# Prompt attention: division of the probabilities moved from VectorE to GpSimd, half of the transposed copies moved to VectorE, copies issued ahead of the exponentials

## The chip, the cores and the metric

The kernel is one launch on one core of one Trainium2 chip. The core has five engines that each run their own instruction list in order and meet only at semaphores: TensorE (PE) for matrix products, VectorE (DVE), ScalarE (ACT), GpSimd (POOL) and SyncE (SP), which only starts transfers. The metric is device microseconds from start to end of the one launch. Before the change three runs took 1468.16, 1467.0 and 1467.94 us, the median is 1467.94 us.

## What is computed

One decoder layer for a prompt of 512 rows and for 8 sequences that decode 4 rows each (32 rows, with a cache of 2048 rows). The layer is a SwiGLU half, a projection into all heads, two kinds of attention, an output projection, a second SwiGLU half and a gated embedding. The part that the change touches is the attention of the prompt: 12 heads of mixer A, which see every key at or before the query with a table of biases, and 4 heads of mixer B, which see the 128 best keys by a separate score. Cut to one head and one block of queries:

```
logits = q @ k.T + bias            # bias holds -1e30 where a key must not be seen
m      = logits.max(-1)
pr     = exp(logits - m)
l      = pr.sum(-1)
o      = (pr / l) @ v
```

The three dilated patterns of mixer A are folded into one softmax by adding the log of how often a key occurs to its bias. Mixer B divides by its own denominator in the same way.

## The kernel before, in words

The dense stages before and after attention work on all 544 rows and are not touched. Prompt attention runs between them and the decode attention. It has 32 steps. Step m takes head pair q = m // 4 (heads 2q and 2q+1) and block of queries i = m % 4, 128 queries each; since a query sees no later key, block i has 128 * (i + 1) keys. So four steps make a group (one head pair) with 128, 256, 384 and 512 key columns. Groups 0 to 5 are mixer A, groups 6 and 7 mixer B. A step goes through these pieces, each for both heads (h2 = 0 and 1):

- `scores(m)` on PE (line 1965) puts q @ k.T into a PSUM bank.
- VectorE adds the bias and takes the row minimum of the negated sum (line 1381), into one of six tiles `LP`, so a tile is free again three steps later.
- ScalarE takes the exponential in place and sums the row (line 931).
- `normalise(m)` on VectorE takes the two reciprocals (line 1358) and scales both tiles (line 1361).
- `transposed(m)` on PE (line 1975) turns the probabilities, 128 x 128 at a time, into two PSUM banks, one for each head.
- ScalarE copies both banks to `PTS` (line 940).
- `values(m)` on PE (line 1987) multiplies with the value rows. After four steps VectorE takes the group's output out (`take_out`, line 1365).

Nothing plans the order; each engine's order is written out. In round m PE does scores(m), transposed(m-2), values(m-3). ScalarE does the exponentials of step m and then the copies of step m-2. VectorE does the logits of step m, then normalise(m-1), and after every fourth step take_out. After the logits of step 10 VectorE also builds the query blocks for decoding (`decode_queries`, lines 1333 to 1350).

GpSimd has two tasks here. After the logits of each of the groups 0 to 5 it issues four transfers that load the bias tables of the head pair after next (`load_bias`, line 666). For the mixer B groups it adds the top-k mask to the bias (`mask_bias`, line 696), for blocks 1 to 3 of each group, and the logits of those blocks wait for that sum in `TM`. `TM` holds one block for each of the two heads, so the next block's sum waits until the logits have read the last one.

Decode attention follows on VectorE's list right behind the last take_out: VectorE starts the top-k rounds of the decode rows (lines 1402, 1403, 1457) there.

## Time and profile before

| | us |
|---|---|
| median of three runs | 1467.94 (1467.0 to 1468.16) |
| profiled execution, its own time | 1468.33 |
| span of the profiled execution | 1466.7 |
| PE busy in the span | 1375.8 (94%) |
| VectorE busy | 551.8 (38%) |
| ScalarE busy | 449.5 (31%) |
| GpSimd busy | 627.5 (43%) |

The span is what the hardware profiler recorded from the first to the last instruction, and 1.6 us of the execution's own time lie outside it. The shares of busy time are means over stages that are limited by different things. Prompt attention covers 641.0 us (the first scores) to 730.5 us (the end of the last take_out), 89.5 us or 6% of the span, and only that stretch tells what the change can do.

### The profile page before, as it was taken

The numbers are of one execution on the slowest core, as the hardware profiler recorded it, in microseconds if no ns is written. First come the engines' busy times: TensorE is split into PE (matmuls) and PEld (weight loads), VectorE is DVE, ScalarE is ACT, GpSimd is POOL, SyncE is SP. The second block draws the span as 40 slices with busy tenths as digits, with TensorE's granted clock in tenths as the row PEclk, the third lists the DMA queues.
The fourth block names the chain that finished last, engine by engine and source line by source line (L and its number), as shares of the span: only waits on it lengthen the run. The fifth ranks groups of instructions, "written<-read, shape, count | busy, mean of one in ns | idle before, by whom it ended". The sixth has DMA issues, their size and how long they took to land.

```text
span 1466.7 us, 30734 instructions
## 1 busy us (share of the span) xinstructions
PE 1375.8 (94%) x12059; PEld 1269.4 (87%) x12059; DVE 551.8 (38%) x1340; ACT 449.5 (31%) x833; POOL 627.5 (43%) x431
## 2 busy tenths in 40 slices
PE   6999999999989999997877897989999999999988
PEld 6999999999979988965555565979999999999888
DVE  5222222200242246777899524162222222110454
ACT  2122222211262333246644431153222222111441
POOL 6343333455465645321455003544333333554642
PEclk9999999999989999999999998989999999999999
DMA  6298755766355533331199898434565657665221
GB/s 231 86 269 316 257 197 208 250 230 213 124 180 170 157 87 102 137 103 53 41 277 283 259 319 312 137 133 167 192 208 192 215 192 269 213 222 173 70 70 47
DMA packets 95775, 269.83 MB, mean 184 GB/s; under 512 B 36306, under 2 KB 36691, under 8 KB 95161
## 3 DMA queue, kind: packets, MB, share of 16 engines
q1 hardware_dynamic: 89000, 255.34, 52.0%
q0 software_dynamic: 5632, 10.50, 2.6%
q10 hardware_dynamic: 1040, 2.62, 1.2%
q8 instruction: 66, 1.08, 0.3%
q14 instruction: 37, 0.30, 0.1%
HBM read 259.78 MB, written 109.10 MB: 252 GB/s over the span
## 4 chain that ended last, share of the span: by engine, by line
PE 81%; DVE 8%; POOL 4%; ACT 2%; issue 2%; DMA 2%; SPq 1%; ACTq 0%; DVEq 0%; POOLq 0%
PE bank L1615 22%; PE bank L1619 21%; PE bank L1617 21%; POOL w_rest L576 2%; DVE idx_scores L1457 2%; DMA cache_a_ring<-in_cache_a 2%; PE bank L1663 1%; PE bank L2158 1%; PE bank L1975 1%; PE bank L1965 1%; PE bank L1665 1%; PE bank L1664 1%; PE bank L1987 1%; DVE idx_scores_left L1403 1%; POOL x_rest L586 1%
## 5 line engine op out<-in xcount | busy, mean ns | idle before, releaser
L576 POOL TENSOR_TENSOR w_rest<-w_raw,w_high 128x1024 fp32r<-128x1024 f32 (+2 forms) x159 | 410.3, 2581 | 596.4 <-ACT w_high L751 595.5
L751 ACT ACTIVATE w_high<-w_raw 128x1024 fp32r<-128x1024 f32 (+2 forms) x159 | 180.2, 1134 | 778.0 <-PE bank L1619 746.0
L1615 PE MATMUL bank<-x_high,w_high 128*128 128x272 f32 x1808 | 378.1, 290 | 13.1 <-POOL x_rest L586 11.7
L1619 PE MATMUL bank<-x_high,w_rest 128*128 128x272 f32 x1808 | 374.6, 289 | 0.0
L1617 PE MATMUL bank<-x_rest,w_high 128*128 128x272 f32 x1808 | 373.4, 288 | 0.0
L1615 PEld LDWEIGHTS bank<-x_high,w_high 128*128 128x128 f32 x1808 | 284.3, 189 | 21.4 <-issue 16.6
L1617 PEld LDWEIGHTS bank<-x_rest,w_high 128*128 128x128 f32 x1808 | 284.8, 189 | 0.0
L1619 PEld LDWEIGHTS bank<-x_high,w_rest 128*128 128x128 f32 x1808 | 282.8, 189 | 0.0
L1058 DVE SCALAR_TENSOR_TENSOR hidden<-silu_gate,bank 128x272 f32<-128x272 f32 x88 | 34.5, 434 | 389.3 <-ACT silu_gate L771 389.3
L1615 PE MATMUL bank<-hidden_high,w_high 128*128 128x272 f32 x616 | 127.7, 288 | 0.0
L1619 PE MATMUL bank<-hidden_high,w_rest 128*128 128x272 f32 x616 | 127.5, 288 | 0.0
L1617 PE MATMUL bank<-hidden_rest,w_high 128*128 128x272 f32 x616 | 127.0, 288 | 0.0
L1615 PEld LDWEIGHTS bank<-hidden_high,w_high 128*128 128x128 f32 x616 | 97.0, 188 | 0.2
L1617 PEld LDWEIGHTS bank<-hidden_rest,w_high 128*128 128x128 f32 x616 | 96.8, 188 | 0.0
L1619 PEld LDWEIGHTS bank<-hidden_high,w_rest 128*128 128x128 f32 x616 | 96.2, 189 | 0.0
L1079 DVE SCALAR_TENSOR_TENSOR y<-y,bank 128x272 f32<-128x272 f32 x42 | 16.5, 434 | 208.1 <-PE bank L1619 179.4
L2032 PE MATMUL bank<-consts_sb,cache_a_ring 128*128 128x128 f32 x336 | 52.5, 297 | 23.9 <-DMA cache_a_ring<-in_cache_a 22.9
L2032 PEld LDWEIGHTS bank<-consts_sb,cache_a_ring 128*128 128x128 f32 x336 | 38.8, 149 | 37.3 <-DMA cache_a_ring<-in_cache_a 31.7
L398 POOL DMA_DIRECT2D kv_b_pages<-in_cache_b x64 | 46.3, 723 | 40.3 <-issue 40.3
L1062 DVE CAST hidden_high<-hidden 128x544 f32 (+1 forms) x44 | 49.1, 1116 | 7.8 <-DVE hidden L1058 3.5
L955 ACT ACTIVATE k_a_t<-bank 128x512 f32<-128x512 f32 x56 | 33.4, 597 | 54.7 <-PE bank L2032 54.7
L718 POOL TENSOR_TENSOR attn_out_rest<-attn_out_t,attn_out_high 128x512 fp32r<-128x512 f32 x8 | 10.5, 1331 | 89.6 <-DVE attn_out_high L1506 89.6
(317 smaller groups left out, 1875.2 us busy)
## 6 DMA issues: line engine op xcount, KB each, us to landing
out_a_sample<-in_cache_a SPq DMA_DIRECT2D x73, 1344.0 KB
w_raw<-in_w_wi SPq DMA_DIRECT2D x88, 512.0 KB, 5.2
cache_a_ring<-in_cache_a SPq DMA_DIRECT2D x112, 384.0 KB, 4.8
w_raw<-in_w_wo SPq DMA_DIRECT2D x32, 704.0 KB, 5.3
w_raw<-in_w_w_in SPq DMA_DIRECT2D x26, 512.0 KB, 3.7
w_raw<-in_w_gate SPq DMA_DIRECT2D x8, 640.0 KB, 3.9
bias_toeplitz<-rev_bias POOLq DMA_DIRECT2D x32, 128.0 KB, 2.6
kv_b_pages<-in_cache_b POOLq DMA_DIRECT2D x64, 64.0 KB, 4.1
```

The source lines that it names most:

```text
L398: eng.dma_start(KVP[:, :, q, :], cache_b[bass.ds(page, 1), :, 0:2 * HD].rearrange("o p (s n) -> (o p) s n", s=2)).then_inc(kv_in[g // 4 + ...
L576: nc.gpsimd.tensor_tensor(rest_part(u0, i, j)[:, 0:tiles, :], RAW[:, slot, 0:tiles, :], high_part(u0, i, j)[:, 0:tiles, :].bitcast(F32), A ...
L751: nc.scalar.activation(high_part(u0, i, j)[:, 0:tiles, :], RAW[:, slot, 0:tiles, :], ACT.Copy).then_inc(S["hi_ready"], 1)
L955: nc.scalar.activation(KTA[:, n % 2, 0:512], BANK[b0][:, :], ACT.Copy)
L1058: last = v.scalar_tensor_tensor(half(HF, s, n), half(SG, s, n), 0.5, BANK[4 * s + 2 + n][:, 0:HALF], ALU.mult, ALU.mult)
L1062: v.tensor_copy(HH[:, bass.ds(c, 1), :], HF[:, s:s + 1, :]).then_inc(S["hh_done"], 1)
L1079: last = v.scalar_tensor_tensor(half(Y, m, n), half(Y, m, n), ALPHA, BANK[2 * (m % 2) + n][:, 0:HALF], ALU.mult, ALU.add)
L1457: own.done(v.match_replace(SC[:], TOP[:, 8 * r:8 * r + 8], SC[:], PASSED))
L1615: mm(banks[n][:, 0:HALF], wh, xh[n], start=start, stop=False)
L1617: mm(banks[n][:, 0:HALF], wh, xl[n], start=False, stop=False)
L1619: last = mm(banks[n][:, 0:HALF], wl, xh[n], start=False, stop=stop)
L2032: last = tr(BANK[2 * (n % 2) + c // 4][:, 128 * (c % 4):128 * (c % 4) + 128], AR[:, n % KEY_RING, 128 * c:128 * c + 128], IDENT)
```

## The change

The reciprocals stay on VectorE, but for the first 24 steps (groups 0 to 5) the scaling by them is done by GpSimd, one instruction for each head, which waits for VectorE's reciprocals through a new semaphore `inv_done`. For the same steps the transposed probabilities of the second head are copied from PSUM by VectorE (`keep_pt`) instead of ScalarE. On ScalarE the copies of step m-2 now stand ahead of the exponentials of step m, in all 32 steps. GpSimd's bias loads stand behind the division of each group's fourth step, and its first two mask sums (group 6, block 1) stand between the divisions of steps 22 and 23. PE's waits follow: `probs_ready` and `pt_kept` name the semaphore of the engine that did the work.

```
+            def divide(m):
+                c, nk = 44 + 2 * m % 6, 128 * (m % 4 + 1)
+                pool.wait_ge(S["inv_done"], m + 1)
+                for h2 in range(2):
+                    l = LP[(2 * m + h2) % 6][:, 0:nk]
+                    nc.gpsimd.tensor_scalar(l, l, SMALL[:, c + h2:c + h2 + 1], None, ALU.mult
+                                            ).then_inc(S["probs_done_p"], 1)
...
-            for q in range(6):
-                pool.wait_ge(S["logits_done"], 8 * (q + 1))
+            for m in range(POOL_STEPS):
+                divide(m)
+                if m % 4 == 3:
+                    for h2 in range(2):
+                        load_bias(m // 4 * 2 + 4 + h2)
+                if m == POOL_STEPS - 2:
+                    for h2 in range(2):
+                        mask_bias(HEADS_A // 2, 1, h2)
...
+            def invert(m):
+                dve.wait_ge(S["exp_done"], 2 * m + 2)
+                c = 38 + 2 * m % 6
+                v.reciprocal(SMALL[:, c + 6:c + 8], SMALL[:, c:c + 2]).then_inc(S["inv_done"], 1)
+
+            def keep_pt(k):
+                nk = 128 * (k % 4 + 1)
+                dve.wait_ge(S["pt_ps"], 2 * k + 2)
+                if k >= 2:
+                    dve.wait_ge(S["pv_done"], 2 * k - 2)
+                v.tensor_copy(PTS[:, k % 2, 1, 0:nk], BANK[3][:, 0:nk]).then_inc(S["pt_sb_d"], 1)
...
-                if m >= 1:
+                if 0 < m <= POOL_STEPS:
+                    invert(m - 1)
+                elif m > POOL_STEPS:
                     normalise(m - 1)
+                if 0 <= m - 2 < POOL_STEPS:
+                    keep_pt(m - 2)
...
-                    pe.wait_ge(S["probs_done"], n + 1)
+                    pe.wait_ge(*probs_ready(n))
                     if m >= 1:
-                        pe.wait_ge(S["pt_sb"], n - 1)
+                        pe.wait_ge(*pt_kept(m - 1, h2))
```

On ScalarE, around the last step of group 4 and the first of group 5, each round of before puts two exponentials ahead of two copies (`logits_96` to `logits_101` are the six `LP` tiles, `probs_t` is `PTS`):

```order
L931 ACTIVATE logits_98,small<-logits_98,small 128x384 [waits logits_done]
L931 ACTIVATE logits_99,small<-logits_99,small 128x384 [waits logits_done]
L940 ACTIVATE probs_t<-bank 128x128 [waits pv_done,pt_ps] x2
L931 ACTIVATE logits_100,small<-logits_100,small 128x512 [waits logits_done]
L931 ACTIVATE logits_101,small<-logits_101,small 128x512 [waits logits_done]
L940 ACTIVATE probs_t<-bank 128x256 [waits pv_done,pt_ps] x2
```

The same place on ScalarE now:

```order
L960 ACTIVATE probs_t<-bank 128x128 [waits pv_done,pt_ps]
L967 ACTIVATE logits_98,small<-logits_98,small 128x384 [waits logits_done]
L967 ACTIVATE logits_99,small<-logits_99,small 128x384 [waits logits_done]
L960 ACTIVATE probs_t<-bank 128x256 [waits pv_done,pt_ps]
L967 ACTIVATE logits_100,small<-logits_100,small 128x512 [waits logits_done]
L967 ACTIVATE logits_101,small<-logits_101,small 128x512 [waits logits_done]
```

The copy of 256 columns has moved from behind the 512-column exponentials to ahead of them, and there is one copy where there were two.

On VectorE, at the fourth step of a group, before (the rows called ISA are the logits and the read-out of their minimum):

```order
L1381 ISA logits_100,small<-bank,bias_toeplitz 128x512 [waits toe_in0,pt_ps,sc_ps]
L1381 ISA small 128x1
L1381 ISA logits_101,small<-bank,bias_toeplitz 128x512 [waits toe_in1,pt_ps,sc_ps]
L1381 ISA small 128x1
L1358 RECIPROCAL small<-small 128x2 [waits exp_done]
L1361 TENSOR_SCALAR logits_98<-logits_98,small 128x384 [waits dve_step]
L1361 TENSOR_SCALAR logits_99<-logits_99,small 128x384
L1365 COPY attn_out_t<-bank 128x512 [waits pv_done]
```

The same place on VectorE now:

```order
L1422 ISA logits_100,small<-bank,bias_toeplitz 128x512 [waits toe_in0,pt_ps,sc_ps]
L1422 ISA small 128x1
L1422 ISA logits_101,small<-bank,bias_toeplitz 128x512 [waits toe_in1,pt_ps,sc_ps]
L1422 ISA small 128x1
L1394 RECIPROCAL small<-small 128x2 [waits exp_done]
L1402 COPY probs_t<-bank 128x256 [waits pv_done,pt_ps]
L1406 COPY attn_out_t<-bank 128x512 [waits pv_done]
```

The reciprocal keeps its place behind the logits of the next step, the two scalings are gone, and a copy that waits for the transposes of the step before stands in their place.

On GpSimd, from the division of step 22 to the mask sums of group 6, block 2, now (before, the four loads came first and the four mask sums followed each other):

```order
L718 TENSOR_SCALAR logits_98<-logits_98,small 128x384 [waits inv_done]
L718 TENSOR_SCALAR logits_99<-logits_99,small 128x384
L709 TENSOR_TENSOR bias_masked<-bias_toeplitz,topk_work 128x256 [waits toe_in0,proj_out,topk_prompt_done]
L709 TENSOR_TENSOR bias_masked<-bias_toeplitz,topk_work 128x256 [waits toe_in1]
L718 TENSOR_SCALAR logits_100<-logits_100,small 128x512 [waits inv_done]
L718 TENSOR_SCALAR logits_101<-logits_101,small 128x512
L679 DMA bias_toeplitz<-rev_bias 64x512 x4
L709 TENSOR_TENSOR bias_masked<-bias_toeplitz,topk_work 128x384 [waits logits_done,toe_in0]
L709 TENSOR_TENSOR bias_masked<-bias_toeplitz,topk_work 128x384 [waits logits_done,toe_in1]
```

The sums of block 2 have moved behind two divisions of 512 columns and the four loads.

## Rows read from the trace of the kernel before

**Rows 1.** Two windows: PE, PEld, DVE, ACT, POOL busy (instructions), PEclk, DMA share, GB/s.
```profile
670.00:680.00 10.00, 7.43 (x59) 5.18 (x60) 6.44 (x27) 6.29 (x19) 2.29 (x4) 0.70 0.19 55
690.00:700.00 10.00, 8.68 (x82) 5.44 (x78) 7.30 (x30) 7.49 (x27) 2.29 (x4) 1.00 0.19 52
```

**Rows 2.** Waits, 640 to 732 us: us in total, times, longest.
```profile
PE bank L1975 <- ACT probs_t L940: 12.5, 8, 5.1
```

**Rows 3.** Timeline, PE: start, us, instruction [idle before it <- releaser].
```profile
672.57 1.51 PE L1975 MATMUL bank<-consts_sb,logits 128*128 128x128 f32 x6 [5.07 <-ACT probs_t L940]
...
688.70 0.44 PE L1975 MATMUL bank<-consts_sb,logits 128*128 128x128 f32 x2
...
692.11 0.49 PE L1965 MATMUL bank<-proj 64*128 64x128 f32 x4
693.92 0.85 PE L1975 MATMUL bank<-consts_sb,logits 128*128 128x128 f32 x6 [1.32 <-ACT probs_t L940]
...
698.59 0.44 PE L1975 MATMUL bank<-consts_sb,logits 128*128 128x128 f32 x2
```

**Rows 4.** Timeline, ACT, 690.4 to 694.2 us.
```profile
692.71 0.71 ACT L931 ACTIVATE logits<-logits,small 128x512 f32<-128x512 f32 x1
...
693.41 0.63 ACT L940 ACTIVATE probs_t<-bank 128x256 f32<-128x256 f32 x2
```

**Rows 5.** Timeline, DVE, 690 to 695 us.
```profile
692.48 0.16 DVE L1358 RECIPROCAL small<-small 128x2 f32<-128x2 f32 x1
692.68 0.75 DVE L1361 TENSOR_SCALAR logits<-logits,small 128x384 f32<-128x384 f32 x2
693.34 0.68 DVE L1365 COPY attn_out_t<-bank 128x512 f32<-128x512 f32 x1
...
694.36 0.16 DVE L1358 RECIPROCAL small<-small 128x2 f32<-128x2 f32 x1
```

**Rows 6.** POOL's groups by shape: line, instruction, count | busy us, mean ns of one.
```profile
L696 POOL TENSOR_TENSOR bias_masked<-bias_toeplitz,topk_work 128x512 f32<-128x512 f32 x4 | 5.1, 1296 | 1.7 <-DVE small L1381 1.7
...
L696 POOL TENSOR_TENSOR bias_masked<-bias_toeplitz,topk_work 128x384 f32<-128x384 f32 x4 | 3.9, 1000 | 2.9 <-DVE small L1381 2.9
L696 POOL TENSOR_TENSOR bias_masked<-bias_toeplitz,topk_work 128x256 f32<-128x256 f32 x4 | 3.3, 835 | 0.9 <-DVE small L1381 0.9
...
L656 POOL TENSOR_SCALAR_AFFINE_SELECT topk_work<-topk_work 128x128 f32<-128x128 f32 x3 | 0.9, 308 | 0.1
...
L642 POOL MEMSET ones<- 128x128 f32 x1 | 0.2, 205 | 0.3 <-POOLq L2342 0.3
...
L2342 POOL MEMSET const-float32-1.0<- 128x1 f32 x1 | 0.1, 99 | 0.0
```

**Rows 7.** Timeline, POOL, 690 to 713 us, and its first two mask sums alone.
```profile
692.86 2.29 POOL L666 DMA_DIRECT2D bias_toeplitz<-rev_bias  x4 [7.60 <-DVE small L1381]
...
704.97 3.61 POOL L696 TENSOR_TENSOR bias_masked<-bias_toeplitz,topk_work 128x256 f32<-128x256 f32 x4
...
704.97 1.69 POOL L696 TENSOR_TENSOR bias_masked<-bias_toeplitz,topk_work 128x256 f32<-128x256 f32 x2
...
...
712.75 0.73 POOL L696 TENSOR_TENSOR bias_masked<-bias_toeplitz,topk_work 128x256 f32<-128x256 f32 x1 [0.90 <-DVE small L1381]
```

**Rows 8.** Timeline, all engines, 688 to 713 us: four rows of DVE.
```profile
706.83 0.42 DVE L1381 CUSTOM_DVE_ANT_0 logits<-bank,bias_masked 128x256 f32<-128x256 f32 x1 [0.41 <-POOL bias_masked L696]
...
709.07 0.55 DVE L1381 CUSTOM_DVE_ANT_0 logits<-bank,bias_masked 128x384 f32<-128x384 f32 x1
...
709.74 2.26 DVE L1361 TENSOR_SCALAR logits<-logits,small 128x256 f32<-128x256 f32 x2
...
712.53 0.08 DVE L1381 DVE_READ_ACCUMULATOR2_ANT small<- 128x1 f32 x1
```

**Rows 9.** The stage behind it: a window as in Rows 1.
```profile
750.00:770.00 20.00, 14.05 (x202) 9.92 (x200) 18.37 (x41) 9.57 (x22) 11.49 (x17) 1.00 0.97 282
```

**Rows 10.** Chain of waits, 728 to 860 us, shares by line.
```profile
by line: DVE idx_scores L1457 19.5%; DMA cache_a_ring<-in_cache_a 10.8%; DVE idx_scores_left L1403 9.7%; DVE topk_lists L1402 8.9%; PE bank L2032 8.5%; PE bank L2015 5.3%; issue 5.2%; PE bank L2158 3.3%; DVE logits_a L1475 2.8%; SPq L398 2.
```

More of the change, by code:

```diff
@@ L271, in build_program @@
             ix_ps ix_relu ix_acc wsel_ps wsel_done kp_t kp_sb kp_sc kp_relu kp_sum kp_row ix_causal
-            topk_prompt_done sc_ps logits_done exp_done den_done probs_done pt_ps pt_sb pv_done o_sb tm_done
+            topk_prompt_done sc_ps logits_done exp_done den_done probs_done  probs_done_p inv_done pt_ps pt_sb pt_sb_d pv_done o_sb tm_done
             new_rows_out proj_out copy_done
@@ L294, in build_program, with probs_ready, pt_kept @@
         N_STEPS = 2 * (HEADS_A + HEADS_B)
+        POOL_STEPS = 2 * HEADS_A
+        def probs_ready(n):
+            if n < 2 * POOL_STEPS:
+                return S["probs_done_p"], n + 1
+            return S["probs_done"], n + 1 - 2 * POOL_STEPS
+        def pt_kept(m, h2):
+            if m >= POOL_STEPS:
+                return S["pt_sb"], POOL_STEPS + 2 * (m - POOL_STEPS) + h2 + 1
+            return S["pt_sb_d" if h2 else "pt_sb"], m + 1
         THIRD = [FIRST[name] + 2 for name in ("w_in", "wi2", "gate")]
@@ L697, in mask_bias @@
                                         MSK[:, i - 1, 0:nk], ALU.add).then_inc(S["tm_done"], 1)
-            for q in range(6):
-                pool.wait_ge(S["logits_done"], 8 * (q + 1))
+            def divide(m):
+                c, nk = 44 + 2 * m % 6, 128 * (m % 4 + 1)
+                pool.wait_ge(S["inv_done"], m + 1)
                 for h2 in range(2):
-                    load_bias(2 * q + 4 + h2)
+                    l = LP[(2 * m + h2) % 6][:, 0:nk]
[9 more added lines that the diff above has]
+                        mask_bias(HEADS_A // 2, 1, h2)
             for q in (6, 7):
                 for i in range(1, 4):
-                    for h2 in range(2):
-                        mask_bias(q, i, h2)
+                    if (q, i) != (6, 1):
+                        for h2 in range(2):
+                            mask_bias(q, i, h2)
             pool.wait_ge(S["ids_in"], 16)
@@ L926, in _ @@
                 for h2 in range(2):
-                    if m < N_STEPS:
-                        n, nk = 2 * m + h2, 128 * (m % 4 + 1)
-                        act.wait_ge(S["logits_done"], n + 1)
-                        l = LP[n % 6][:, 0:nk]
-                        nc.scalar.activation(l, l, ACT.Exp, bias=SMALL[:, 32 + n % 6:33 + n % 6], scale=-1.0,
-                                             accum_out=SMALL[:, 38 + n % 6:39 + n % 6]).then_inc(S["exp_done"], 1)
-                for h2 in range(2):
-                    if m >= 2:
+                    if m >= 2 and (h2 == 0 or m - 2 >= POOL_STEPS):
                         k = m - 2
@@ L941, in _ @@
                                              ).then_inc(S["pt_sb"], 1)
+                for h2 in range(2):
+                    if m < N_STEPS:
+                        n, nk = 2 * m + h2, 128 * (m % 4 + 1)
+                        act.wait_ge(S["logits_done"], n + 1)
+                        l = LP[n % 6][:, 0:nk]
+                        nc.scalar.activation(l, l, ACT.Exp, bias=SMALL[:, 32 + n % 6:33 + n % 6], scale=-1.0,
+                                             accum_out=SMALL[:, 38 + n % 6:39 + n % 6]).then_inc(S["exp_done"], 1)
             def exp_a(a):
@@ L1981, in values @@
                     pe.wait_ge(S["o_sb"], q - 1)
-                pe.wait_ge(S["pt_sb"], 2 * m + 2)
+                for h2 in range(2):
+                    pe.wait_ge(*pt_kept(m, h2))
                 for j in range(i + 1):
```

## The prediction, made before the result was known

> **What bounds the kernel now.** The page says PE is busy for 94% of the span, so prompt attention (89.5 us) counts only if PE waits in it. I read the waits of that stretch first: PE's transposes waited 12.5 us, in 8 waits, for ScalarE's copy of the transposed probabilities [rows 2]. The windows say that no engine is full there: in ten steady microseconds PE is busy 8.68, VectorE 7.30, ScalarE 7.49, GpSimd 2.29 [rows 1]. So what sets the pace is a chain between engines. PE's timeline shows its place: once in a group, at the transposes of the group's third step (384 columns), PE stands 1.32 us [rows 3], and one of these waits, behind VectorE's decode_queries, is 5.07 us, after which a window shows the granted clock at 0.70 [rows 1, 3]. ScalarE's timeline shows why: the copy that PE needs starts at 693.41, right behind a 512-column exponential that began at 692.71 [rows 4], though the transposes it copies were long done. A group lasts 9.89 us: its first step's transposes start at 688.70, those of the next group at 698.59 [rows 3].
>
> What happens to a microsecond won or lost here: VectorE starts the decode top-k right behind the last take_out, it is busy 18.37 of 20 us in the next stage [rows 9], and its top-k lines lead the chain there (19.5, 9.7 and 8.9%) [rows 10]. So the end of the stage moves the end of the kernel one for one.
>
> **Copies ahead of exponentials.** The copy of 256 columns would be done by about 692.4, and the 1.32 us wait for ScalarE goes. What is late next is the division of the same step, since its reciprocals stand behind the logits of the fourth step: they end at 692.48 + 0.16 = 692.64 [rows 5]. With VectorE still scaling, the first head would be ready at 692.68 + 0.35 and PE would start near 693.2 instead of 693.92.
>
> **Division on GpSimd.** No row shows this operation, so I bound it. Below: writing alone, 205 ns for 128 columns and 99 for one [rows 6], 0.83 ns for a column, so 0.21, 0.42 and 0.52 us for 128, 384 and 512 columns. Above: the sums of two tiles, 0.84, 1.00 and 1.30 us for 256, 384 and 512 [rows 6], which leaves 0.45 for 128. Nearest is the select of 128 columns, which reads one tile and writes one: 308 ns [rows 6]. I take its 0.31 and the column price of the memset: 0.31, 0.41, 0.52, 0.63 us. The Trainium skill (GPSIMD Engine Reference, section 4.1, Engine selection) has one-input elementwise work on GpSimd near line rate, and two-input work about twice as slow as VectorE; by that the lower bound would be nearer. No run here shows it.
>
> Crossing engines costs too. Into GpSimd: VectorE's read-out ends at 712.61 and the sum that waits for it starts at 712.75, 0.14 [rows 7, 8]. Out of it: two sums end at 704.97 + 1.69 = 706.66 and VectorE starts at 706.83, 0.17 [rows 7, 8].
>
> Third step of a group. First head ready at 692.64 + 0.14 + 0.52 + 0.17 = 693.47, second at 693.99. Before, they were started at 693.92 and, three transposes of 0.10 later (six take 0.85, two 0.44 [rows 3]), at 694.23. The second head decides: 0.25 to 0.3 won. The same sum holds behind decode_queries, because there too the transposes come 1.28 us after the reciprocals. Five times (groups 1 to 5): -1.3.
>
> First step of the next group. The reciprocals of the fourth step end at 694.52 [rows 5]. Then 0.14, two divisions of 0.63, four loads of together 2.29 [rows 7], two divisions of 0.31 and 0.17: the second head is ready at 699.00, where before PE started it near 698.70 (698.59 [rows 3] plus one transpose). So the loads, which cost nothing before, now stand ahead of a division and give back 0.3, five times: +1.5, less the lead that the group brings along, about 0.2 in two of them: +1.2.
>
> Group 0. The pipeline fills and only a short wait goes: -0.3.
>
> Into mixer B. GpSimd now does, after the reciprocals of step 22: 0.14, two divisions of 0.52, two mask sums (1.69), two divisions of 0.63, four loads (2.29), two mask sums of 384 columns (3.61 - 1.69 = 1.92 [rows 7]): 8.3 us. Before, these sums ended at 708.58 [rows 7], 6.05 after the reciprocals (one group behind 692.64, at 702.53). They are 2.3 later. VectorE's logits of the second head took them at 709.07 [rows 8], 0.5 of slack, and about 0.3 is the lead: +1.5. From there VectorE sets the pace, with scalings that a sum on GpSimd stretches from about 0.62 to 2.26 for a pair [rows 8], so the lag isn't made up.
>
> **Edits priced at nothing.** VectorE's 24 copies replace 48 scalings: a copy of 512 from PSUM takes 0.68 and a pair of 384 scalings 0.75 [rows 5], so VectorE has no more to do than now. Behind each copy stand the logits of the next step, but PE does the transposes that the copy waits for ahead of those scores, so no new order arises. If that cover went, a step would lose a copy, 0.3 to 0.68. PE's additional waits are for work done long before. In groups 6 and 7 copies ahead help only where VectorE isn't the one waited for: 0 to -0.4, I take -0.1.
>
> **Sum.** -1.3 + 1.2 - 0.3 + 1.5 - 0.1 = +1.0 us on the execution's own 1468.33, which lies 0.39 above the median; against the median, 1467.94 + 1.0 = 1468.9.
>
> **Rivals.** GpSimd divides at the price of a two-tile sum (slower). Place: the same two waits. At 1.00 for 384 the second head comes at 692.64 + 0.14 + 2.00 + 0.17 = 694.95, 0.7 later than now, and GpSimd's work in a group, 2 x (0.45 + 0.84 + 1.00 + 1.30) + 2.29 = 9.5 us with waits on top, passes the group's 9.89: about +2 a group. Five groups, and 2 x (0.48 + 0.67) more into mixer B (+3.8 there): about +13, 1481. It decides from about 0.75 us for 512 columns on (0.15 more for each division adds about 0.3 at each of the two places). Halfway, at 0.73 for 384 and 0.93 for 512 (the select's price with nearly all of it by column), the second head comes at 694.41, 0.2 late, and the first step of the next group 0.8 late at the end of it: five times +0.6 to +0.7, and +2.5 into mixer B, less 0.3, about +5, 1473. For it: all large rows of GpSimd are of that kind. Against it: they read two tiles, and the select is cheaper.
>
> GpSimd divides nearly as VectorE does (faster). At 0.35 for 384 and 0.43 for 512 the second head is ready at 693.65, 0.6 won, nothing is lost to the loads, and the way into mixer B costs 0.7 to 1.0: 5 x -0.6 - 0.3 + 0.7 = -2.6. If the shorter stall behind decode_queries also keeps the clock of that group up (it runs at 0.70 of full speed in 670 to 680 us now [rows 1]), another 1 to 1.5: about -4, 1464. Against it: it takes less than the select's own fixed part.
>
> The change leaves the wait where it is. It would if ScalarE's order stayed; the order shows it doesn't.
>
> **How the numbers follow.** Forecast 0.46, slower rival 0.34 (most of it between +3 and +8, about 0.1 at +9 and beyond), faster rival 0.20. A measurement of this kernel tells about 0.2%, 2.9 us, from no change: that is 1465.0 to 1470.9, and the forecast with its lower bound of price (-1.3) lies inside it. So faster 0.20, same 0.46, slower 0.34. The forecast's own range is 1466 to 1471. The range that leaves out 2 in 10 reaches to most of both rivals: 1464.0 to 1477.0.
>
> **What would show it.** In the profile after: PE's wait at the third step's transposes turns from ScalarE's copy to GpSimd's division and is still 0.8 to 1.0 us for the first head, with a second, short one ahead of the second head; GpSimd's rows show about 0.5 us for 384 and 0.63 for 512 columns; a group lasts 9.7 to 10.0 us; VectorE's wait for the mask sum of group 6 grows from 0.41 to 1.5 or more; the last take_out ends near 731.5 instead of 730.5. It is wrong if GpSimd's 512 columns take over 0.75 or under 0.45 us, if a group lasts under 9.4 or over 10.4, or if the stage's end moves by more than 3 us.

## The result: 1.2% slower, outside the predicted range

Six runs of the changed kernel have a median of 1485.09 us (1483.85 to 1492.3), six runs of the kernel before on the same chip 1468.05. The ratio is 1.0121, with a 95% interval of 1.0102 to 1.014: about 17.8 us slower, 15.0 to 20.6. The forecast was 1468.9 with a range up to 1477.0. The profiled execution of the changed kernel took 1485.67 us, its span is 1484.0.

Where the time went is seen in the starts of `take_out`, the copy with which VectorE ends a group:

| us | group 0 | 1 | 2 | 3 | 4 | 5 | 6 | 7 |
|---|---|---|---|---|---|---|---|---|
| before | 658.34 | 671.99 | 683.46 | 693.34 | 703.24 | 714.47 | 724.93 | 729.85 |
| after | 658.70 | 674.12 | 688.05 | 701.87 | 715.63 | 732.55 | 742.56 | 746.95 |

A steady group (2 to 3) went from 9.89 us to 13.82, the interval into mixer B (from 4 to 5) from 11.23 to 16.92, and groups 6 and 7 became 1.0 us shorter together (10.01 and 4.39 after 10.46 and 4.92). The stage ends 17.1 us later, the span is 17.3 longer: what the stage loses passes to the end one for one, as [rows 9, 10] had it. One pair of executions shows this only roughly: over the profiled executions of the twelve kernels below, the growth of the span is between 1.2 us less and 4.1 us more than the delay of the last `take_out`. The chain of waits by line from 745 to 877 us leads with VectorE's top-k lines as in [rows 10], at the same shares:

```profile
by line: DVE idx_scores L1502 19.5%; DMA cache_a_ring<-in_cache_a 10.2%; DVE idx_scores_left L1448 9.7%; DVE topk_lists L1447 8.9%; issue 6.5%; SPq L410 4.7%; SPq L411 4.5%; PE bank L2078 3.8%; PE bank L2204 3.7%; SPq L524 2.9%; DVE logits_
```


The waits of the changed kernel from 640 to 749 us (in total, times, longest), which answer to [rows 2]:

```profile
ACT probs_t L960 <- PE bank L2020: 49.4, 33, 3.6
PEld bank L2020 <- POOL logits L718: 30.9, 36, 4.3
...
DVE probs_t L1402 <- PE bank L2020: 19.6, 14, 2.1
PE bank L2020 <- POOL logits L718: 16.4, 21, 4.1
```

PE's transposes no longer wait for ScalarE's copy. They wait for GpSimd, 16.4 us in 21 waits, and ScalarE and VectorE now wait for the transposes (PEld is PE's loading of weights, which waits along with it).

GpSimd's groups by shape in the same stretch (count | busy us, mean ns of one), which answer to [rows 6]:

```profile
L718 POOL TENSOR_SCALAR logits<-logits,small 128x512 f32<-128x512 f32 x12 | 18.6, 1562 | 0.0
L718 POOL TENSOR_SCALAR logits<-logits,small 128x384 f32<-128x384 f32 x12 | 14.8, 1242 | 9.5 <-DVE small L1394 9.5
...
L718 POOL TENSOR_SCALAR logits<-logits,small 128x256 f32<-128x256 f32 x12 | 10.9, 921 | 8.2 <-DVE small L1394 8.2
...
L718 POOL TENSOR_SCALAR logits<-logits,small 128x128 f32<-128x128 f32 x12 | 7.2, 610 | 12.6 <-DVE small L1394 12.5
L709 POOL TENSOR_TENSOR bias_masked<-bias_toeplitz,topk_work 128x512 f32<-128x512 f32 x4 | 5.1, 1294 | 1.7 <-DVE small L1422 1.7
```

This is the price on which the experiments turn. The division takes 0.61, 0.92, 1.24 and 1.56 us, where 0.31, 0.41, 0.52 and 0.63 were assumed: 2.48 ns for each column, (1562 - 610) / 384. The longest of the twelve divisions of 512 columns took 1565 ns, where the mean is 1562, so the work of the other engines beside them leaves no mark on the price. It is dearer than the sum of two tiles of the same width (1294 ns), which was taken as its upper bound.

GpSimd's timeline of one group, which answers to [rows 7]:

```profile
687.91 5.54 POOL L718 TENSOR_SCALAR logits<-logits,small 128x384 f32<-128x384 f32 x4 [0.89 <-DVE small L1394]
693.40 2.10 POOL L679 DMA_DIRECT2D bias_toeplitz<-rev_bias  x4
695.52 1.19 POOL L718 TENSOR_SCALAR logits<-logits,small 128x128 f32<-128x128 f32 x2
```

And PE's, which answers to [rows 3]:

```profile
689.21 0.55 PE L2020 MATMUL bank<-consts_sb,logits 128*128 128x128 f32 x3 [0.91 <-POOL logits L718]
690.42 0.90 PE L2020 MATMUL bank<-consts_sb,logits 128*128 128x128 f32 x3 [0.67 <-POOL logits L718]
691.26 1.12 PE L2033 MATMUL bank<-probs_t,v_prompt 128*64 128x128 f32 x8
692.31 1.23 PE L2010 MATMUL bank<-proj 64*128 64x256 f32 x4
693.47 1.97 PE L2020 MATMUL bank<-consts_sb,logits 128*128 128x128 f32 x8
695.37 1.55 PE L2033 MATMUL bank<-probs_t,v_prompt 128*64 128x128 f32 x12
696.85 0.92 PE L2010 MATMUL bank<-proj 64*128 64x384 f32 x4
```

The third step's two divisions and the fourth step's two run back to back. PE gets the two heads of the third step 1.2 us apart and waits for each. The six transposes that took 0.85 together in [rows 3] take 0.55 for the first head and 0.90 for the second, and everything behind them up to 696.8 us is slow as well: the eight transposes of the fourth step take 1.97 us. The windows, which answer to [rows 1], show the clock:

```profile
670.00:680.00 10.00, 5.61 (x32) 3.37 (x31) 6.13 (x41) 3.16 (x10) 6.02 (x5) 0.65 0.01 2
690.00:700.00 10.00, 9.57 (x61) 6.10 (x61) 3.41 (x13) 4.20 (x15) 7.68 (x11) 0.66 0.19 55
```

From 690 to 700 us VectorE is busy 3.41 us instead of 7.30, and PE's granted clock is 0.66 instead of 1.00 (1.00 is 2.4 GHz; the clock has two levels, 2.4 and 1.2 GHz, and the window shows their mean).

### The profile page after: what moved, and what is told of

It is laid out like the page before. It is cut to its first block, busy times and chain, and to the rows that moved or that the text cites. A ratio compares the mean times of both kernels' runs of the same rounds, so it can differ in the third digit from the quotient of the medians.

```text
span 1484.0 us, 30760 instructions
## 1 busy us (share of the span) xinstructions
PE 1383.5 (93%) x12059; PEld 1270.1 (86%) x12059; DVE 545.9 (37%) x1316; ACT 443.0 (30%) x809; POOL 676.7 (46%) x479
## 4 chain that ended last, share of the span: by engine, by line
PE 80%; DVE 7%; POOL 6%; issue 2%; DMA 2%; ACT 1%; SPq 1%; ACTq 0%; DVEq 0%; POOLq 0%
PE bank L1660 22%; PE bank L1664 21%; PE bank L1662 21%; POOL logits L718 2%; POOL w_rest L589 2%; DVE idx_scores L1502 2%; DMA cache_a_ring<-in_cache_a 2%; PE bank L1708 2%; PE bank L2204 1%; PE bank L1710 1%; PE bank L1709 1%; PE bank L2033 1%; PE bank L2020 1%; PE bank L2010 1%; DVE idx_scores_left L1448 1%
## 5 line engine op out<-in xcount | busy, mean ns | idle before, releaser
L718 POOL TENSOR_SCALAR logits<-logits,small 128x128 f32<-128x128 f32 (+3 forms) x48 | 51.3, 1084 | 30.4 <-DVE small L1394 30.2
L2020 PEld LDWEIGHTS bank<-consts_sb,logits 128*128 128x128 f32 x160 | 21.4, 168 | 40.7 <-POOL logits L718 30.9
L2020 PE MATMUL bank<-consts_sb,logits 128*128 128x128 f32 x160 | 35.1, 343 | 19.2 <-POOL logits L718 16.4
```

Source lines behind the costliest of these rows:

```text
L718: nc.gpsimd.tensor_scalar(l, l, SMALL[:, c + h2:c + h2 + 1], None, ALU.mult).then_inc(S["probs_done_p"], 1)
L2020: last = tr(BANK[2 + h2][:, 128 * j:128 * j + 128], LP[n % 6][:, 128 * j:128 * j + 128], IDENT)
```

## The experiments

The kernel before ran beside each of them. In the last three columns of the table, "of before" is the ratio to it with its 95% interval, and the groups are read from the starts of `take_out` in the one profiled execution (the interval from group 2 to 3, and from 4 to 5 into mixer B).

| kernel | median us | of before | group | into B |
|---|---|---|---|---|
| before | | 1 | 9.89 | 11.23 |
| after | 1485.09 | 1.0121 (1.0102 to 1.0140) | 13.82 | 16.92 |
| 1 copies ahead alone | 1463.62 | 0.9968 (0.9950 to 0.9986) | 9.15 | 11.23 |
| 2 division on VectorE | 1469.56 | 1.0008 (0.9992 to 1.0025) | 9.89 | 12.69 |
| 3 by a constant | 1491.55 | 1.0167 (1.0136 to 1.0198) | 12.32 | 16.51 |
| 4 two-tile form | 1472.79 | 1.0034 (1.0011 to 1.0056) | 10.38 | 13.97 |
| 5 loads on SyncE | 1486.59 | 1.0129 (1.0098 to 1.0161) | 13.65 | 16.95 |
| 6 old order on ScalarE | 1491.17 | 1.0139 (1.0106 to 1.0172) | 13.82 | 16.93 |
| 7 ahead, third division first | 1460.57 | 0.9939 (0.9915 to 0.9963) | 8.60 | 11.30 |
| 8 two-tile form, loads on SyncE | 1473.26 | 1.0021 (1.0004 to 1.0039) | 10.06 | 13.10 |
| 9 short divisions | 1471.90 | 1.0015 (0.9996 to 1.0034) | 9.49 | 12.67 |
| 10 short, loads on SyncE | 1469.75 | 1.0011 (0.9992 to 1.0030) | 9.50 | 11.90 |
| 11 second division first too | 1467.04 | 0.9991 (0.9974 to 1.0008) | 9.33 | 11.50 |
| 12 waits of PE filled | 1486.60 | 1.0121 (1.0095 to 1.0147) | 12.87 | 16.69 |

My theory after the result was that the price of GpSimd's division carries nearly all of the loss. The rivals were VectorE's copies, ScalarE's new order, the loads that stand ahead of a division, and the clock.

### One part of the change at a time

**1, the kernel before with copies ahead of exponentials.**

```
                 for h2 in range(2):
-                    if m < N_STEPS:
-                        act.wait_ge(S["logits_done"], n + 1)
...
-                for h2 in range(2):
                     if m >= 2:
                         act.wait_ge(S["pt_ps"], n + 1)
...
+                for h2 in range(2):
+                    if m < N_STEPS:
+                        act.wait_ge(S["logits_done"], n + 1)
...
```

> The kernel before with one part of the change alone: ScalarE's copies of the probabilities stand ahead of the step's exponentials; both heads stay ScalarE's, the divisions stay VectorE's and the loads stay where they were. Theory A (the division's price on GpSimd carries the whole loss, and the other parts are small): 3 to 5 us faster than before, since in a group's third step the transposes no longer wait for ScalarE's copy. Theory B (the new order on ScalarE costs time by itself, because the next step's exponentials come later): 2 us or more slower than before.

Measured: 0.9968, 4.7 us faster (2.1 to 7.3). Theory A. A group became 0.74 us shorter, and groups 6 and 7 together 1.1 us.

**2, the changed kernel with the division back on VectorE, and GpSimd's loads and mask sums in their old place.**

```
-                if 0 < m <= POOL_STEPS:
-                    invert(m - 1)
-                elif m > POOL_STEPS:
+                if m >= 1:
                     normalise(m - 1)
```

> The changed kernel with the 48 divisions of the first 24 steps back on VectorE, and with them the old place of GpSimd's bias loads and masks; VectorE still copies the second head's probabilities and the copies still stand ahead of the exponentials. Theory A (the loss is GpSimd's division): within 3 us of the kernel before, so about 14 to 18 us faster than the changed kernel. Theory B (VectorE's copies, which wait for TensorE's transposes in the middle of VectorE's queue, lengthen the step): 8 us or more slower than before.

Measured: 1.0008, 1.2 us (-1.2 to +3.7) and no difference from before that can be told: the loss goes with the division. VectorE's copies are not free either, though: against experiment 1 this kernel gives the whole gain back (9.89 us in a group instead of 9.15), since VectorE now divides and copies. Its window of 690 to 700 us, with VectorE busy 8.79 of 10 instead of the 7.30 of [rows 1]:

```profile
690.00:700.00 10.00, 9.09 (x79) 5.39 (x76) 8.79 (x36) 6.51 (x21) 2.21 (x4) 1.00 0.19 53
```

**6, the changed kernel with ScalarE's old order.**

```
                 for h2 in range(2):
+                    if m < N_STEPS:
+                        act.wait_ge(S["logits_done"], n + 1)
...
                     if m >= 2 and (h2 == 0 or m - 2 >= POOL_STEPS):
                         act.wait_ge(S["pt_ps"], n + 1)
...
-                for h2 in range(2):
-                    if m < N_STEPS:
-                        act.wait_ge(S["logits_done"], n + 1)
...
```

> The changed kernel with ScalarE's old order, exponential of a head ahead of its copy. Theory A (the chain runs through GpSimd's divisions, so ScalarE's order no longer decides): within 2.5 us of the changed kernel. Theory B (with copies ahead, the exponentials and with them GpSimd's input come late, and the new order is part of the loss): 4 us or more faster than the changed kernel. A third outcome, 4 us or more slower, would say that the new order still gains within the changed kernel what it gains in the kernel before.

Measured: the steady groups last 13.82 and 13.75 us, as in the changed kernel, and the ratios (1.0139 and 1.0121, 2.6 us apart) agree within their intervals. Theory A. The order that shortens a steady group of the kernel before by 0.74 us gains nothing in one here, because the copies wait for transposes that wait for GpSimd. Group 6, in which GpSimd divides nothing, takes 10.46 us again, as in the kernel before.

### The price of the division

**3, a constant in place of the row's reciprocal.**

```
-                    nc.gpsimd.tensor_scalar(l, l, SMALL[:, c + h2:c + h2 + 1], None, ALU.mult
+                    nc.gpsimd.tensor_scalar(l, l, 0.5, None, ALU.mult
```

> The changed kernel, but GpSimd multiplies the probabilities by the constant 0.5 in place of the row's reciprocal; this leaves out the division by the row's sum and nothing else. Theory A (the division is dear because GpSimd reads a multiplier for each row): the 512-column instruction falls from 1.56 us to 0.6 to 1.0 us and the kernel ends 0 to 6 us above before. Theory B (the dear thing is GpSimd's pass over the columns itself): the 512-column instruction stays at 1.4 to 1.6 us and the kernel stays 14 to 18 us above before.

**4, the same division as a product of two tiles.**

```
-                    nc.gpsimd.tensor_scalar(l, l, SMALL[:, c + h2:c + h2 + 1], None, ALU.mult
+                    nc.gpsimd.tensor_tensor(l, l, SMALL[:, c + h2:c + h2 + 1].broadcast_to([128, nk]), ALU.mult
```

> The changed kernel with the same division written as a product of two tiles on GpSimd, the second one the reciprocal's column repeated along the row. Theory A (the form of the instruction sets its price, and the two-tile form costs what the two-tile sums of this kernel do, 1.30 us for 512 columns): 512 columns take about 1.3 us and the kernel ends 9 to 14 us above before, 3 to 8 us faster than the changed kernel. Theory B (any pass of GpSimd over these tiles in this stage costs 1.5 us or more, say because other engines hold the memory): no faster than the changed kernel.

GpSimd's groups by shape, first of experiment 3, then of experiment 4, widest and narrowest form:

```profile
L718 POOL TENSOR_SCALAR logits<-logits 128x512 f32<-128x512 f32 x12 | 17.7, 1494 | 0.0
...
L718 POOL TENSOR_SCALAR logits<-logits 128x128 f32<-128x128 f32 x12 | 6.3, 544 | 12.6 <-DVE small L1394 12.5
```

```profile
L718 POOL TENSOR_TENSOR logits<-logits,small 128x512 f32<-128x512 f32 x12 | 12.2, 1040 | 0.0
...
L718 POOL TENSOR_TENSOR logits<-logits,small 128x128 f32<-128x128 f32 x12 | 4.6, 412 | 12.5 <-DVE small L1394 12.5
```

The constant takes 2.47 ns for a column, (1494 - 544) / 384, as the reciprocal's 2.48, so reading a multiplier for each row costs only 0.07 us an instruction; theory A of experiment 3 falls. The two-tile form, which was expected at 1.30, takes 1.04 for 512 columns and 1.64 ns for a column, and the kernel ends 5.0 us above before (1.6 to 8.2), 13 us faster than the changed kernel and better than either theory gave. So the form of the instruction sets its price, and the form with one tile and a multiplier is the dear one. The group of experiment 3 is 1.5 us shorter than the changed kernel's: GpSimd is busy 9.98 us in it instead of 10.61, and the granted clock was 1.00 instead of 0.75 (see experiment 12). Yet its time is no better: 1.0167, 24.5 us above before, more than either theory gave. Its profiled execution was the fastest of four, 1485.61 us; there the stage ended at 743.7 us, 3.9 ahead of the changed kernel's, with the same span. The four were lost behind the stage, where both run the same instructions (experiment 2 lost 3.1 there against before). Why stays open.

**9, GpSimd divides only as many columns as cost the assumed price.**

```
-                    l = LP[(2 * m + h2) % 6][:, 0:nk]
+                    l = LP[(2 * m + h2) % 6][:, 0:(8, 48, 93, 137)[m % 4]]
```

> The changed kernel, but GpSimd's division takes in only the first 8, 48, 93 and 137 columns of the 128, 256, 384 and 512; this leaves the other columns undivided. By the line through the changed kernel's four forms (0.29 us and 2.48 ns for each column) the instructions then take the 0.31, 0.41, 0.52 and 0.63 us that the prediction had assumed, and everything else stays. Theory A (the prediction's other terms hold, and its only wrong one is the price of the division): a group of 9.5 to 10.2 us and the kernel -1 to +3 us from before. Theory B (the change would have lost even at that price, by the way through GpSimd's queue and semaphores or by VectorE's copies): 5 us or more slower than before.

GpSimd's groups by shape of experiment 9:

```profile
L718 POOL TENSOR_SCALAR logits<-logits,small 128x137 f32<-128x137 f32 x12 | 7.4, 631 | 2.1 <-DVE small L1394 2.1
L718 POOL TENSOR_SCALAR logits<-logits,small 128x93 f32<-128x93 f32 x12 | 6.2, 526 | 15.2 <-DVE small L1394 15.2
L718 POOL TENSOR_SCALAR logits<-logits,small 128x48 f32<-128x48 f32 x12 | 4.8, 413 | 9.8 <-DVE small L1394 9.8
L718 POOL TENSOR_SCALAR logits<-logits,small 128x8 f32<-128x8 f32 x12 | 3.6, 315 | 13.2 <-DVE small L1394 13.1
```

The prices came out as assumed, and with them the kernel is 2.2 us from before (-0.6 to +5.0), where the prediction's sum was +1.0. Theory A: of the loss of 17.8 us some 15.6 are the difference in price, with all that follows from it, the lower clock among it.

### The loads ahead of a group's first division

**5, 8 and 10, the loads of heads 4 to 15 issued by SyncE**, in the changed kernel, in that of experiment 4 and in that of experiment 9.

```
-                if m % 4 == 3:
-                    for h2 in range(2):
-                        load_bias(m // 4 * 2 + 4 + h2)
...
+            for q in range(6):
+                sp.wait_ge(S["logits_done"], 8 * (q + 1))
+                for h in (2 * q + 4, 2 * q + 5):
+                    for p in range(0, 128, REV_COPIES):
...
+                        sp.dma_start(TOE[p:p + REV_COPIES, h % 4, :], rows).then_inc(toe_sp[h % 4], 16)
```

> The changed kernel with the bias loads of heads 4 to 15 issued by SyncE, which is idle in this stage, so that GpSimd goes from one division to the next. Theory A (the loss is time on GpSimd's queue, and the loads that stand ahead of a group's first division add to it): a group falls from 13.8 us to about 12.5 to 13, and the kernel is 4 to 8 us faster than the changed kernel. Theory B (the loads lie in time that GpSimd has anyway): within 1.5 us of the changed kernel.

> The changed kernel with the two-tile form of the division, which took 1.04 us for 512 columns in the fourth experiment, and the loads issued by SyncE. Theory A (GpSimd's queue is what bounds the group, so its busy time of 5.8 + 2.1 us in a group of 10.38 is still felt): a group falls to 9.3 to 9.9 us and the kernel ends 2 to 6 us faster than the fourth experiment, near the kernel before. Theory B (once the division is short, the path runs through VectorE's reciprocals and TensorE): within 1.5 us of the fourth experiment.

> The kernel of the shortened divisions with the loads of heads 4 to 15 issued by SyncE, which tests the prediction's term of 1.2 us in a group for the loads that stand ahead of a group's first division (again it leaves part of the columns undivided). Theory A (the term is right): a group is 0.8 to 1.5 us shorter than with the shortened divisions alone and the kernel 4 to 7 us faster than that one. Theory B (the loads lie beside other work, as the 0.17 us in a group of the fifth experiment say for the long divisions): less than 0.4 us in a group, and within 2 us of the kernel of the shortened divisions.

Measured: a group is 0.17 us shorter in experiment 5 (13.65 for 13.82), 0.32 in 8 (10.06 for 10.38), and not shorter at all in 10 (9.50 for 9.49). None of the three times differs from its partner's by more than the intervals allow. So in a steady group the loads cost nothing with the short divisions and little with the dearer ones: theory B in 5 and 10, and in 8 less than the 0.5 to 1.1 us that theory A expected. (The expectation of experiment 10 has the prediction's term wrong: it was 0.2 to 0.3 us in each of five groups, 1.2 in all, not 1.2 in a group. 9.50 for 9.49 leaves no room for that either.) On the way into mixer B the loads do count: 11.90 for 12.67 in 10, 13.10 for 13.97 in 8, and nothing in 5. The reason for the steady group stands in PE's timeline of experiment 9:

```profile
695.22 0.88 PE L2033 MATMUL bank<-probs_t,v_prompt 128*64 128x128 f32 x12
696.02 0.92 PE L2010 MATMUL bank<-proj 64*128 64x384 f32 x4
696.87 0.44 PE L2020 MATMUL bank<-consts_sb,logits 128*128 128x128 f32 x2
```

GpSimd's first two divisions of the group run from 696.14 to 696.74 there, behind the loads. The transposes that need them stand on PE behind the values of the third step and the scores of the next group's third step, and PE reaches them at 696.87 without a wait, 0.13 us after the second division.

### The clock

**12, PE's two waits at the third step's transposes filled with transposes of the identity.**

```
-                    pe.wait_ge(*probs_ready(n))
                     if m >= 1:
                         pe.wait_ge(*pt_kept(m - 1, h2))
+                    if m < POOL_STEPS and m % 4 == 2:
+                        for j in range((7, 4)[h2]):
+                            tr(BANK[2 + h2][:, 0:128], IDENT, IDENT)
+                    pe.wait_ge(*probs_ready(n))
```

> The changed kernel, in which TensorE fills its two waits at the transposes of a group's third step (0.91 and 0.67 us, for GpSimd's two divisions) with 7 and 4 additional transposes of the identity matrix; they go to the part of the bank that the real transposes overwrite, so the result stays. Theory A (the clock that falls behind these waits is part of the loss: 8 transposes then take 1.97 us in place of 1.09, 12 value products 1.55 in place of 0.88): the windows of the steady groups show a granted clock of 0.9 to 1.0 in place of 0.75, a group falls from 13.8 to 12.3 to 13.2 us, and the kernel is 3 to 7 us faster than the changed kernel. Theory B (the lower clock only fills time in which TensorE would wait for GpSimd): within 1.5 us of the changed kernel, whatever the clock. If the clock stays at 0.75 with the waits filled, the fall has another reason than these waits.

One steady group as a window, first of the changed kernel, then of experiment 12:

```profile
688.00:701.90 13.90, 12.02 (x80) 7.39 (x78) 6.29 (x27) 6.37 (x21) 10.69 (x13) 0.75 0.14 40
```

```profile
689.80:702.70 12.90, 11.14 (x94) 7.14 (x95) 6.35 (x27) 6.20 (x21) 10.67 (x13) 1.00 0.16 43
```

With the waits filled the clock stays at 1.00 in this group (2.4 GHz) and it lasts 12.87 us, 0.95 less, though PE has 11 transposes more to do. Experiment 3 points to the same size: its group at 1.00 lasts 12.32 us, and with the 0.63 us that GpSimd is busy less in it that makes 12.95, by estimate. So the lower clock costs the steady group of the changed kernel about a microsecond, as theory A says.

What brings the clock down, and when that costs time, is less clear. Two groups of experiment 3 as windows, and PE's waits in them, which nothing fills:

```profile
686.30:698.60 12.30, 9.39 (x78) 5.46 (x76) 6.30 (x26) 6.16 (x21) 9.97 (x13) 1.00 0.16 45
698.60:710.90 12.30, 10.56 (x76) 6.32 (x76) 6.20 (x26) 6.28 (x21) 9.98 (x13) 0.86 0.16 44
```

```profile
687.36 0.55 PE L2020 MATMUL bank<-consts_sb,logits 128*128 128x128 f32 x3 [0.99 <-POOL logits L718]
688.49 0.55 PE L2020 MATMUL bank<-consts_sb,logits 128*128 128x128 f32 x3 [0.59 <-POOL logits L718]
...
699.67 0.55 PE L2020 MATMUL bank<-consts_sb,logits 128*128 128x128 f32 x3 [1.35 <-POOL logits L718]
700.81 0.90 PE L2020 MATMUL bank<-consts_sb,logits 128*128 128x128 f32 x3 [0.59 <-POOL logits L718]
```

In the first, PE stands 0.99 and 0.59 us and the clock stays up; in the second it falls, and the group is no longer for it. In experiment 12 itself the clock was down from group 1 to 2 (0.75 from 680 to 690 us), and that interval took 13.90 us, as in the changed kernel (13.93). So filling the waits kept the clock up in the two steady groups, but that these waits alone bring it down is not shown.

The sum does not show the gain: the ratio is the same 1.0121 as the changed kernel's, which is theory B's outcome. The two groups from 2 to 4 were 1.9 us shorter, which the interval of 3.8 us either way cannot tell; in the profiled execution group 0 ended 1.7 us later, and group 6 took 1.6 us more (11.59, at a clock of 0.85). What the clock cost the whole kernel is therefore not measured, only that it was about 1 us in a steady group.

### What the result points to

**7, experiment 1 with the third step's division ahead of the fourth step's logits; 11, the second step's division ahead of the third step's logits as well.**

Experiment 7 against experiment 1 (experiment 11 has `i >= 2` and `i < 2` in the two conditions):

```
+                if i == 3:
+                    normalise(m - 1)
                 for h2 in range(2):
                     n, h = 2 * m + h2, 2 * q + h2
...
-                if m >= 1:
+                if m >= 1 and i != 3:
                     normalise(m - 1)
```

> The kernel before with ScalarE's copies ahead of the exponentials, as in the first experiment, and VectorE's divisions of the third step put ahead of the fourth step's two logits. Theory A (the third step's transposes, of 384 columns for each head, wait for these divisions, and the fourth step's logits have time): 0.5 to 1.5 us faster than the first experiment, so 5 to 6.5 us faster than before. Theory B (the fourth step's logits are as urgent, for they release ScalarE's longest exponentials): as the first experiment or 1 to 3 us slower than it.

> As the seventh experiment (the kernel before, copies ahead of exponentials, third step's divisions ahead of the fourth step's logits), and also the second step's divisions ahead of the third step's logits. Theory A (the transposes of each step wait for its divisions): a group falls from 8.60 us by another 0.2 to 0.6 us, and the kernel is 1 to 3 us faster than the seventh. Theory B (in the third step the logits are the ones waited for, since ScalarE's exponentials follow on them at once): 0 to 4 us slower than the seventh.

Experiment 7 beats both kernels: 0.9939, 9.0 us faster than before (5.4 to 12.5), more than the expected 5 to 6.5 by its median. A steady group is 0.55 us shorter than in experiment 1; the largest part, 2.6 us, lies in the profiled executions between group 1 and 2 (9.01 for 11.64), where the granted clock was 0.88 instead of 0.77. The window over one group shows why the order has no more to give in a steady group:

```profile
685.30:693.90 8.60, 8.60 (x79) 5.41 (x78) 7.16 (x32) 7.35 (x25) 2.06 (x4) 1.00 0.22 64
```

PE is busy for 8.60 of 8.60 us at full clock. Experiment 11 goes past the optimum: a group of 9.33 us. Its waits from 664 to 735 us:

```profile
ACT logits L940 <- DVE small L1383: 11.5, 10, 4.3
...
DVE small L1358 <- ACT logits L940: 9.2, 9, 2.0
```

VectorE, with the logits held back, waits for exponentials (0.9 us in experiment 7), and ScalarE for the logits (5.7 there). In the third step the logits are the urgent ones, theory B. The loss against experiment 7 is 7 to 8 us by the two ratios, larger than it gave, and 3.9 from group 0 to 7 in the two profiled executions.

## Why the prediction was wrong

**The step that failed is the price of the division on GpSimd.** No row of before showed it, and I bounded it from rows of other forms: a memset and a select from below and beside, a two-tile sum from above. The upper bound was none. One tile and a multiplier cost 1.56 us for 512 columns, two tiles 1.29, two tiles of which one repeats a column 1.04. The select of 128 columns (308 ns in [rows 6]), which I took as nearest, was half of what the division of 128 columns took (610). For 128 columns the upper bound of 0.45 does not even follow from its rows: a line through the sums of 256 and 512 columns gives 0.60. The slower rival had the right place, the two waits at the third step, but its price stopped at 1.30.

The Trainium skill (GPSIMD Engine Reference, section 4.1, Engine selection) has one-input elementwise work on GpSimd near line rate and two-input work about twice as slow as VectorE. The runs differ: the one-input division took 1562 ns (1494 with a constant) where VectorE's same form took 484 in this trace, 3.2 times as long, and it was the two-input form that was cheaper. The measurement decides.

VectorE's row for that comparison, steps 24 to 31 of the changed kernel:

```profile
L1388 DVE TENSOR_SCALAR logits<-logits,small 128x512 f32<-128x512 f32 x4 | 1.8, 484 | 0.1
```

A steady group's 3.9 us then come apart like this: -0.40 from before to experiment 9, which is the whole change at the assumed price; +3.38 from there to experiment 12, which is the price (and that experiment's 11 additional transposes); +0.95 from there to the changed kernel, which is the clock.

**What bounds the kernel** was read rightly: a chain between engines whose tight place is the third step's transposes. Experiment 1 takes out the wait for ScalarE's copy and gains 4.7 us; the changed kernel takes it out too and puts a longer one in. The prediction held the size of that gain: with VectorE still scaling it let PE start at 693.2 instead of 693.92, 0.7 us, and experiment 1 measured 0.74 in a group. Beside its own 0.25 to 0.3 for the whole change this already says that moving the division costs time even at the assumed price; experiment 9, at that price, keeps 0.40 of the 0.74.

**The sign that came true by luck.** PE's wait for the first head was forecast at 0.8 to 1.0 us and is 0.91, though the division takes 1.24 us instead of 0.52. PE itself comes to this place 0.5 us after the reciprocals (688.30 and 687.82), where before it came with them (692.60 and 692.64).

**Third step, -1.3 in five groups, and first step, +1.2.** With the assumed price (experiment 9) the four intervals from group 0 to 4 changed by -0.87, +0.24, -0.40 and -0.40, together -1.4. That is about the first term alone, though not as five equal parts of 0.26. The second, the loads ahead of the division, was wrong: experiment 10 gives it as 0.0 in a steady group. I followed GpSimd's queue to the end of the division and compared it with the start of the transposes before, but the whole group, and with it PE's list ahead of these transposes, had moved as well.

**Into mixer B, +1.5.** At the assumed price it is 12.67 - 11.23 = +1.4, and the wait that the step named is there: VectorE stands 1.6 us for the mask sums in experiment 9, where [rows 8] had 0.41, and with the loads off GpSimd's queue (experiment 10) the interval is 0.8 shorter. VectorE's wait in experiment 9 from 664 to 735 us:

```profile
DVE logits L1422 <- POOL bias_masked L709: 1.6, 2, 1.2
```

The step held at the assumed price. At the real price it is +5.7 and another mechanism. VectorE does not wait for the mask sums at all; it waits for PE's scores, behind the transposes that wait for GpSimd:

```profile
721.14 0.42 DVE L1422 CUSTOM_DVE_ANT_0 logits<-bank,bias_masked 128x256 f32<-128x256 f32 x1 [1.65 <-PE bank L2010]
...
726.66 0.56 DVE L1422 CUSTOM_DVE_ANT_0 logits<-bank,bias_masked 128x384 f32<-128x384 f32 x1 [2.36 <-PE bank L2010]
```

**Group 0, -0.3, and groups 6 and 7, -0.1.** The last two became 1.0 us shorter together, with the same granted clock of 1.00 and in experiments 1 and 2 as well (1.1 and 1.0), so the copies ahead were worth ten times what I took. Group 0 can't be judged: its `take_out` starts between 654.4 and 660.4 us in the profiled executions.

**Crossing engines.** Out of GpSimd I took 0.17, from GpSimd to VectorE. Here the first division ended at 687.91 + 1.24 = 689.15 and PE started at 689.21: 0.06.

**Edits priced at nothing.** In the changed kernel VectorE's copies lie in time that it has: the logits behind one still wait 1.65 us for PE's scores. Where VectorE divides and copies (experiment 2), they cost 0.74 us in a group, the whole gain of the new order. No run takes the copies alone out of the changed kernel.

**The clock** was priced only as a gain of the faster rival. A wait put into PE's list should have been priced with what can come behind it: the next few microseconds of matmuls at the lower clock, 0.95 us in a steady group here.

**The sensitivity came out in its sum, in part by luck.** The halfway rival gave +5 us, 1473, for prices of 0.73 and 0.93. Experiment 4, at 0.83 and 1.04, took 1472.79. Into mixer B it is +2.7 (13.97 for 11.23), near the rival's +2.5; but the four intervals from group 0 to 4 gave +0.5 together, where the rival had 0.6 to 0.7 in each group, and the profiled execution lost 3.1 more in groups 6 and 7, where the granted clock was 0.76 and 0.71. So the sum failed mainly through one input, and the chain that it followed held in the main and not in every term.

## What to carry to other kernels

An operation that moves to an engine on which no row shows the same form has no upper bound from another form, however much heavier that form looks; the range has to stay open upwards until one run has measured it. When several edits come together, run the cheap one alone first: here an exchange of two loops was worth 5 us, and with one more exchange 9, while the part that moved work between engines turned that gain into a loss of 18. And once one engine's queue is taken as late, move all other queues with it before a second lateness is charged.

## What the runs showed of the hardware that I had not expected

On GpSimd one tile times a multiplier is dearer (2.48 ns for a column of 128 float32 rows, and 2.47 with a constant) than the product with a second tile that repeats one column (1.64); the sum of two full tiles lies between, (1296 - 835) / 256 = 1.80 by [rows 6] and (1294 - 768) / 256 = 2.05 in the changed kernel.

The lower clock makes the same group of mixer B 2.7 us longer. Group 6, in which GpSimd divides nothing, as a window of experiment 9 and then of experiment 10, whose work there is the same:

```profile
713.70:726.70 13.00, 11.23 (x71) 6.97 (x72) 10.01 (x31) 7.37 (x23) 4.50 (x4) 0.74 0.00 1
```

```profile
710.50:720.80 10.30, 8.37 (x71) 5.03 (x72) 10.16 (x30) 7.21 (x23) 4.50 (x4) 1.00 0.01 2
```

At a granted clock of 0.74 it took 13.0 us and at 1.00 it took 10.3; PE's 71 matmuls were busy for 11.23 us instead of 8.37. Experiments 4 and 12 lie in line with it, 12.67 us at 0.76 and 11.59 at 0.85. A single profiled execution can carry such a difference, so I read terms of less than 3 us from intervals in the steady groups and not from the time of one execution.
